# Scan stage: table t stored in the order in which it is loaded, in four transfers, and two weight blocks fetched later

## The reference, cut to what matters

```python
D_MODEL, SEQ, CHUNK = 2048, 256, 64
S5_GROUP, S5_GROUPS, S5_STATE = 16, 128, 64

for layer in range(2):
    u = rmsnorm(h, norm_mix[layer])
    h = h + (even_mixer(u, ...) if layer % 2 == 0 else s5_mixer(u, ...))
    h = h + conv_ffn(rmsnorm(h, norm_ffn[layer]), ...)      # up (D x 2*5504), conv, gate, down (5504 x D)
out = rmsnorm(h, norm_final)

def s5_mixer(u, lam_re, lam_im, log_dt, b_re, b_im, c_re, c_im, d, w_glu, b_glu):
    lam_bar = exp(lam * dt)                                  # a complex pole per group and state
    b_bar = ((lam_bar - 1.0) / lam)[..., None] * b
    # per group of 16 channels, along the sequence:
    x[t] = lam_bar * x[t - 1] + b_bar @ u[t]
    y[t] = real(c @ x[t]) + d * u[t]
    y = gelu(y)
    return y * sigmoid(y @ w_glu + b_glu)
```

## Time and profile before

| | us |
|---|---|
| median of 3 runs | 2127.45 (2126.91 to 2128.45) |
| the profiled execution | 2128.25 |
| its span, first to last instruction | 2126.5 |

### The profile page before, as it was taken

The page is one execution under the profiler, slowest core; times in us unless marked ns, Lnnn a source line. Parts: engine busy times, 40 slices in busy tenths (PEclk is TensorE's granted clock), DMA queues, the critical chain, the costliest instruction groups (busy, mean ns, idle before and its releaser), DMA issues.

```text
span 2126.5 us, 40592 instructions
## 1 busy us (share of the span) xinstructions
PE 2050.5 (96%) x13014; PEld 1782.2 (84%) x13014; DVE 1580.7 (74%) x2215; ACT 1108.6 (52%) x1588; POOL 601.8 (28%) x686
## 2 busy tenths in 40 slices
PE   5999999999999999999999878999999999999997
PEld 4888877888888888888888777888888888888886
DVE  7786555877878888878777676888888888865555
ACT  5454344546666656655555414566666666544442
POOL 8993000870000000019888483300000000002121
PEclk9999999999999999999999989999999999999999
DMA  4564433556666555557777884555555555556664
GB/s 164 175 198 166 149 124 104 178 169 207 209 213 205 190 188 187 187 166 223 232 230 233 274 238 146 178 188 187 187 188 187 188 188 192 186 180 178 197 183 135
DMA packets 147162, 398.79 MB, mean 188 GB/s; under 512 B 23184, under 2 KB 48400, under 8 KB 147104
## 3 DMA queue, kind: packets, MB, share of 16 engines
q1 hardware_dynamic: 126176, 379.17, 55.4%
q10 hardware_dynamic: 20928, 18.88, 2.9%
HBM read 377.02 MB, written 18.87 MB: 186 GB/s over the span
## 4 chain that ended last, share of the span: by engine, by line
PE 88%; DVE 5%; issue 2%; DMA 2%; ACT 1%; POOL 1%; ACTq 0%; DVEq 0%; SPq 0%; POOLq 0%
PE bank L331 49%; PE bank L330 25%; PE bank L327 3%; DVE lo L309 2%; PE bank L1736 1%; PE bank L1738 1%; PE bank L1737 1%; PE bank L328 1%; PE bank L1765 1%; DMA rot<-s_rot 1%; DMA uu<-yg 0%; PE bank L1983 0%; PE bank L1887 0%; ACT th L1149 0%; DVE sumt L345 0%
## 5 line engine op out<-in xcount | busy, mean ns | idle before, releaser
L309 DVE TENSOR_TENSOR lo<-raw,hi 128x1024 fp32r<-128x1024 f32 x698 | 898.0, 1295 | 135.5 <-ACT hi L302 121.9
L302 ACT ACTIVATE hi<-raw 128x1024 fp32r<-128x1024 f32 x698 | 731.4, 1056 | 396.2 <-PE bank L331 332.9
L331 PE MATMUL bank<-aa,hi 128*128 128x512 f32 x2588 | 908.6, 393 | 0.0
L331 PE MATMUL bank<-xx,hi 128*128 128x512 f32 x2236 | 784.6, 393 | 0.0
L330 PE MATMUL bank<-aa,lo 128*128 128x256 f32 x2588 | 726.0, 281 | 2.8 <-DVE lo L309 2.8
L330 PE MATMUL bank<-xx,lo 128*128 128x256 f32 x2236 | 626.6, 280 | 1.0 <-DVE lo L309 1.0
L331 PEld LDWEIGHTS bank<-aa,hi 128*128 128x128 f32 x2588 | 487.4, 188 | 102.6
L330 PEld LDWEIGHTS bank<-aa,lo 128*128 128x128 f32 x2588 | 488.8, 189 | 9.9 <-DVE lo L309 3.8
L331 PEld LDWEIGHTS bank<-xx,hi 128*128 128x128 f32 x2236 | 420.1, 188 | 87.7
L330 PEld LDWEIGHTS bank<-xx,lo 128*128 128x128 f32 x2236 | 421.7, 189 | 8.2 <-DVE lo L309 1.6
L340 ACT ACTIVATE lowt<-bank 128x256 f32<-128x256 f32 x212 | 81.3, 383 | 255.5 <-PE bank L331 250.9
(11 more groups left out here) (333 smaller groups left out, 1945.1 us busy)
## 6 DMA issues: line engine op xcount, KB each, us to landing
raw<-in_up SPq DMA_DIRECT2D x344, 512.0 KB, 3.2
raw<-in_down SPq DMA_DIRECT2D x160, 448.0 KB, 4.0
raw<-in_w_in SPq DMA_DIRECT2D x98, 512.0 KB, 3.9
raw<-in_w_out SPq DMA_DIRECT2D x32, 512.0 KB, 3.5
raw<-in_down SPq DMA_DIRECT2D x32, 512.0 KB, 3.6
raw<-in_glu SPq DMA_DIRECT2D x32, 512.0 KB, 3.2
s_c<-cp ACTq DMA_DIRECT2D x16, 256.0 KB, 4.9
s_p<-ut ACTq DMA_DIRECT2D x32, 128.0 KB, 5.1
```

The lines of the kernel that those rows point to most:

```text
L302: A.activation(hi[:, s, :], raw[:, s, :], ACT.Copy).then_inc(hi_done, 1)
L309: V.tensor_tensor(lo[:, s, :], raw[:, s, :], hi[:, s, :].bitcast(f32), SUB).then_inc(lo_done, 1)
L331: last = TE.matmul(bank[:, :], hi[:, s, w], x2(k)[:, :, :], start=False, stop=k == total - 1)
```

## The change

The table in DRAM, `s5_t`, gets the order of the load: (x, j, m, n) with 1 KB for each (x, j). The load of a tile is then 128 contiguous kilobytes. The store is made in four, one for each m, each of 32 partitions by 4 pieces of 256 bytes; every wait on `s5_dma_t` counts 64 per tile in place of 16. The two fetches of the gated unit's blocks 2 and 3 move from behind tiles 8 and 11 to behind tiles 13 and 15, the last one of the scan.

```diff
-        s5_t = nc.dram_tensor("s5_t", [KT, P, T5 * S5_P * T5], f32, kind="Internal").ap()
+        s5_t = nc.dram_tensor("s5_t", [KT, S5_P * 2, T5, 4, S5_P * T5], f32, kind="Internal").ap()
@@ load_t
-                sp.wait_ge(s5_dma_t, 16 * (kt + 1))
+                sp.wait_ge(s5_dma_t, 64 * (kt + 1))
                 if kt >= SLOTS:
                     sp.wait_ge(y_done, kt - SLOTS + 1)
-                sp.dma_start(t_op[:, s, :, :], s5_t[kt, :, :].rearrange("(m x) (j n) -> (x j) m n", m=4, j=T5)
-                             ).then_inc(t_full[s], 16)
+                sp.dma_start(t_op[:, s, :, :].rearrange("p m n -> p (m n)"),
+                             s5_t[kt, :, :, :, :].rearrange("x j m n -> (x j) (m n)")).then_inc(t_full[s], 16)
@@ loads of the scan
-                if kt in (8, 11):
-                    fetch(B_GLU, 4, 0, kt // 3, w[kt // 3, :, :], BW)
+                if kt in (13, 15):
+                    fetch(B_GLU, 4, 0, (kt - 9) // 2, w[(kt - 9) // 2, :, :], BW)
@@ store_p_t
-                    a.wait_ge(s5_dma_t, 16 * kt)
+                    a.wait_ge(s5_dma_t, 64 * kt)
...
-                a.dma_start(s5_t[kt, :, :], k_win[:, :, :, :].rearrange("p j c r -> p (j c r)")).then_inc(s5_dma_t, 16)
+                rows_of = 2 * S5_P
+                for m in range(4):
+                    a.dma_start(s5_t[kt, :, :, m, :],
+                                k_win[rows_of * m:rows_of * (m + 1), :, :, :].rearrange("p j c r -> p j (c r)")
+                                ).then_inc(s5_dma_t, 16)
@@ tile 10 of the scan, on ACT
-                    a.wait_ge(s5_dma_t, 16 * KT)
+                    a.wait_ge(s5_dma_t, 64 * KT)
```

## The result

| | before | after |
|---|---|---|
| median of 20 runs each, us | 2127.72 | 2130.85 |
| profiled execution's span, us | 2126.5 | 2129.1 |
| PE's last turn of the down loop starts | 1207.85 | 1207.54 |
| POOL's first product of the scan | 1220.81 | 1224.62 |
| POOL's product of tile 15 | 1283.45 | 1284.81 |

The ratio is 1.0016, with an interval of 1.0009 to 1.0023: the change costs 3.1 us, 0.16%, where the sum had forecast 1.0 us less. The time lies inside the range, and on the other side of the kernel before than the sum said.

A forecast was written before the change was run, and what follows sets the result against it. PE was taken to bound the down loop, late hand-over from loads to DVE, POOL and PE the scan. 0 + 2.4 - 0.2 - 2.4 - 2.0 + 1.2 = -1.0 us gave 2126.4 us; range 2121.5 to 2133.0.

The forecast's parts named there:

- the sum: Whole kernel: all the forecast's terms added, -1.0 us, giving 2126.4 us; chance 0.36.
- part 1: Down loop: four t stores add 2.6 us per tile on ACT, hidden by PE's matmuls; cost 0, ends 0 and +7.
- The ring: Down loop: load, ACT's split, DVE's low half, next load; forecast to close about 0.2 us short of PE's 16.1 us tile.
- rival A: Down loop: load-and-split cycle outlasts PE's tile, from about 2.8 us added on ACT per tile; 2132.4 us; chance 0.20.
- Part 2: Border between down loop and scan: last t store piece issued 2.5 us later, POOL's start +2.4 us, ends +1.7 and +4.4.
- rival C: Border: small stores as slow per packet as 2 KB ones, 2.0 us more on tile 14's store; 2128.4 us; chance 0.10.
- Part 3: Scan: t loads in 1 KB packets save 0.24 us per tile; -0.2 us before the stalls, 0.8 and 0.4 within them.
- Part 4: Scan: moving two gated-unit blocks, with shorter t loads, shrinks the two stalls by 2.4 and 2.0 us.
- rival D: Scan: stalls are the y transfers' doing, each shrinks by only 1.2 us; 2128.4 us; chance 0.15.
- B: Scan: rival that both stalls vanish, POOL then setting the pace; -5.4 us, 2122.1 us; chance 0.19.
- The y transfer: End of scan: block 3 issued just before y of tiles 8 to 11 delays it, +1.2 us, ends 0 and +1.8.
- The end: Behind the scan: the difference passes whole to the end, as that stage's chain has no wait for a DMA.

## Why the prediction was wrong

The sum said -1.0 and +3.1 came. Two steps together turned the sign: the cost of 0 for the four stores in the loop (part 1), without which the border would have lost less than forecast; and the gain in the scan, forecast as 4.6 us and measured as 2.45 (parts 3 and 4). Either miss alone would have left the kernel within about 1.2 us of the one before.

**Part 1, cost 0: the step that failed first.** The numbers in it held. ACT's idle time before line 302 is 4.7 to 5.1 us (said: 5.2), PE's windows are full, PE loses 0.7 us over the loop. The ring does close, closer than "0.2 us short": rival A's mechanism, without its price. But I asked only whether PE waits, and took a yes or no of it for the cost. ACT is pushed back against PE until it is 1.3 us ahead in place of 3.8, and is late by 2.2 us where the loop ends and PE's matmuls no longer cover it. The kernels with late stores show it: the same stores, ACT at 3.8 us again, and the border back to 13.11 and 12.31 us. The point from which it decides was also off: an addition of 2.4 us per tile uses up the lead and has PE wait a little, where rival A said 2.8; one of 1.5 doesn't.

**Part 2, +2.4: the term is right for what it counted, and mis-sized.** The last piece of tile 14 is issued 2.3 us after the first (1211.23 - 1208.90) and lands after 5.65 us in place of 6.18; from the first store of tile 14 to the copy of tile 15 it is 8.1 us (said: 8.7; before 6.3). So of +4.0 at that copy 1.8 are part 2's own and 2.2 part 1's inheritance; at POOL's start it is +3.8. The +3.8 lie inside the ends given for the term (+1.7 to +4.4), but that is luck: the upper end was drawn for rival C, which the packets' landing excludes. The rates behind the four stores, given about a microsecond of room, cost DVE 1.34 us.

**Part 3: the mechanism held alone, and not in company.** -1.4 forecast in all, -1.8 measured for the load by itself (0.4 to 4.3), at 55 ns a packet in place of 41 to 50; by this price the terms give only -0.9. In the changed kernel the -0.2 of the first tiles is +1.2 (from POOL's first product to that of tile 5 it takes 20.00 us, before 18.82). Of it 0.7 are small waits for DVE, 0.74 and 1.14 us in place of 0.25 and 0.93, and 0.6 are the first product itself, 3.33 us in place of 2.77. What makes these longer is open. This is 1.4 of the 2.15 us by which the scan missed.

**Part 4: -1.8 and -1.8 for -2.4 and -2.0.** Right in kind, and 0.8 too much; what is late next was PE's states, not rot. Together with part 3's missing share the sixteen tiles gave -2.45 in place of -4.6. How firm the 1.8 are is less clear than it looks: in the kernels with late stores, where the fetches are moved too, the second stall was as long as before or longer. Of rival D, that the stalls are y's doing, half is true; its 2.4 us for both stalls are a little further from the 3.6 than the sum's 4.4. B failed: none of the stalls vanished.

**The y transfer, +1.2.** 8.95 us for the 9 forecast (a close hit for a time that was 6.5 to 10.1 us in the ten kernels without the wait), and the +1.2 in full on the path to the gated unit.

**The end.** The gated unit's first matmul is 2.57 us later and the span 2.6 longer: what the scan loses passes whole to the end, as said.

## To carry to other kernels

When work is put on an engine that runs ahead of the bottleneck in a loop, ask for two numbers, not one: does the bottleneck wait, and how far is that engine ahead when the loop ends. The lead that it loses is paid at the next border, once; a bottleneck that looks full (here 16.00 of 16 us) doesn't show it. And a transfer that is at the end of a stage's chain should be compared with what is issued beside it before anything else is: a wait of one instruction that let it land first gained 2.4 us by itself and 5.6 with the moved blocks, where neither half of the change gained anything clear of noise. And before a stall of a single trace is priced to half a microsecond, look at how far it differs between two kernels that are equal there.

## What the runs showed of the hardware

The issue of a store on ACT's queue had a median of 0.61 us for 32 partitions with four pieces of 256 bytes each (three dimensions) and 0.36 for the same bytes in one piece per partition (two dimensions), each over 64 stores. Two dimensions with 128 partitions of 1 KB took 0.48, so it isn't settled how much of the difference is the third dimension and how much the number of pieces. For a queue in front of compute work this was worth more than the packets' size: the landings of the two had the same median, 3.9 us, and the same longest, 5.7. Packets that are read cost 18.8 ns of one engine's time at 256 bytes, 55 at 1 KB and 82 at 2 KB, each from one window. And a transfer from SBUF to SBUF (the slowest of the four pieces of the y of tiles 8 to 11) took 6.5 to 10.1 us to land beside weight loads, in ten kernels; with the loads held back it took 3.7 to 4.4, in three.
